# Hybrid decoder layer in split float32: one of the four weight-block sums of a block pair made by an accumulating transfer

## What is computed

```
x <- LN(alpha*x + 0.5*SwiGLU_pre(x))          # w_gate, w_up: 1024 x 2816, w_down: 2816 x 1024
x <- LN(alpha*x + W_out[attention(x) || conv group(x)])
x <- LN(alpha*x + 0.5*SwiGLU_post(x))
swiglu(x) = (silu(x @ wg) * (x @ wu)) @ wd
```

## Time and profile before

| | us |
|---|---|
| median of 3 runs | 1032.84 |
| lowest, highest | 1032.51, 1033.01 |
| the profiled execution's own time | 1032.17 |
| its span in the profile | 1030.4 |
| PE busy | 990.4 (96%) |
| DVE busy | 687.4 (67%) |
| ACT busy | 466.8 (45%) |
| POOL busy | 69.8 (7%) |

### The profile page before, as it was taken

The page is one execution under the profiler, slowest core; times in us unless marked ns, Lnnn a source line. Parts: engine busy times, 40 slices in busy tenths (PEclk is TensorE's granted clock), DMA queues, the critical chain, the costliest instruction groups (busy, mean ns, idle before and its releaser), DMA issues.

```text
span 1030.4 us, 18173 instructions
## 1 busy us (share of the span) xinstructions
PE 990.4 (96%) x7538; PEld 967.2 (94%) x7538; DVE 687.4 (67%) x984; ACT 466.8 (45%) x780; POOL 69.8 (7%) x80
## 2 busy tenths in 40 slices
PE   8979999999999999999999998979999999999994
PEld 8979999999999999999888998979999999999994
DVE  5788742577886468726667687988634587784456
ACT  4455531245445235546555456644521354553230
POOL 2000000000000000107142000000000000000004
PEclk9999999999999999999999999999999999999998
DMA  9255333123225344362022463042432222336402
GB/s 259 83 122 141 108 119 103 42 88 119 82 83 167 100 123 83 100 191 82 23 62 83 133 188 97 28 131 79 132 104 62 83 82 83 103 117 184 146 1 87
DMA packets 131594, 108.19 MB, mean 105 GB/s; under 512 B 13138, under 2 KB 129590, under 8 KB 131496
## 3 DMA queue, kind: packets, MB, share of 16 engines
q1 hardware_dynamic: 130368, 105.46, 34.5%
q10 hardware_dynamic: 1144, 1.57, 1.2%
HBM read 103.08 MB, written 4.95 MB: 105 GB/s over the span
## 4 chain that ended last, share of the span: by engine, by line
PE 71%; DVE 18%; ACT 6%; issue 4%; DMA 0%; DVEq 0%; POOL 0%; ACTq 0%; SPq 0%
PE banks L1057 26%; PE banks L1070 24%; PE banks L880 15%; DVE w_lo L1814 4%; DVE more_raw L1806 2%; DVE w_raw L1806 2%; ACT w_hi L1380 2%; DVE w_sum L1806 2%; PE banks L1242 1%; DVE w_lo L1783 1%; DVE ln_sq L1923 1%; DVE more_lo L1814 1%; ACT w_hi L1366 1%; ACT x_hi L1515 1%; PE banks L1288 1%
## 5 line engine op out<-in xcount | busy, mean ns | idle before, releaser
L1070 PE MATMUL banks<-h_hi,w_hi 128*128 128x280 f32 (+1 forms) x480 | 139.1, 290 | 0.0
L1070 PE MATMUL banks<-h_hi,w_lo 128*128 128x280 f32 (+1 forms) x480 | 139.0, 290 | 0.0
L1070 PE MATMUL banks<-h_lo,w_hi 128*128 128x280 f32 (+1 forms) x480 | 138.8, 289 | 0.0
L880 PE MATMUL banks<-x_hi,w_hi 128*128 128x280 f32 (+1 forms) x416 | 126.1, 303 | 2.9 <-DVE x_lo L2159 0.9
L1057 PE MATMUL banks<-x_hi,w_hi 128*128 128x280 f32 (+1 forms) x400 | 117.9, 295 | 10.6 <-ACT ln_sq L1471 8.7
L880 PE MATMUL banks<-x_lo,w_hi 128*128 128x280 f32 (+1 forms) x416 | 120.6, 290 | 0.0
L880 PE MATMUL banks<-x_hi,w_lo 128*128 128x280 f32 (+1 forms) x416 | 120.5, 290 | 0.0
L1057 PE MATMUL banks<-x_hi,w_lo 128*128 128x280 f32 (+1 forms) x400 | 116.9, 292 | 0.0
L1057 PE MATMUL banks<-x_lo,w_hi 128*128 128x280 f32 (+1 forms) x400 | 116.8, 292 | 0.0
L1783 DVE TENSOR_TENSOR w_lo<-w_raw,w_hi 128x1024 fp32r<-128x1024 f32 (+1 forms) x66 | 77.9, 1183 | 57.6 <-ACT w_hi L1366 57.2
L1057 PE MATMUL banks<-t_hi,w_hi 128*128 128x280 f32 x336 | 98.3, 293 | 0.7 <-issue 0.7
(11 more groups left out here) (238 smaller groups left out, 2654.4 us busy)
## 6 DMA issues: line engine op xcount, KB each, us to landing
w_raw<-in_ffn_w_down SPq DMA_DIRECT2D x30, 512.0 KB, 4.1
more_raw<-in_ffn_w_down SPq DMA_DIRECT2D x28, 512.0 KB, 3.8
w_raw<-in_ffn_w_gate SPq DMA_DIRECT2D x24, 512.0 KB, 4.0
w_raw<-in_ffn_w_up SPq DMA_DIRECT2D x24, 512.0 KB, 5.0
more_raw<-in_ffn_w_gate SPq DMA_DIRECT2D x20, 512.0 KB, 4.0
more_raw<-in_ffn_w_up SPq DMA_DIRECT2D x20, 512.0 KB, 5.1
w_raw<-in_w_in SPq DMA_DIRECT2D x14, 512.0 KB, 4.5
w_raw<-in_w_out SPq DMA_DIRECT2D x32, 128.0 KB, 2.9
```

Of the source, the lines that this page charges most:

```text
L880: mm = nc.tensor.matmul(out[:, 0:n], w[:, t, :], x(k), start=(k == ends[0] and w is hi and x is rhs_hi), stop=(k == ends[1] and w is lo))
L1070: mm = nc.tensor.matmul(out, w[:, k - k0, c * P:(c + 1) * P], h[:, k, cols(half, f)], start=(k == 0 and w is hi and h is h_hi), stop=(ku = ...
```

## The change

S1 is no longer made by DVE. As soon as a21 has landed, POOL issues two transfers that read a22's bytes from DRAM again (256 KB each, two of the four rows of 1 KB of each partition) and add them to a21 in its buffer. DVE makes the other three sums from S1: S2 = S1 - a11, S3 = a22 - S2, S4 = a12 - S2. For j > 0 all three stand ahead of the lo half of step 2's weights. The loads by SP stay as they are, and PE's and ACT's order too.

```
@@ block_hi (ACT)
+                elif s == 3:
+                    act.wait_ge(s1_summed[j % 2], 32 * ((N_PAIRS * f + j) // 2 + 1))
                 else:
-                    act.wait_ge(blocks_summed, 4 * (N_PAIRS * f + j) + ({4: 1, 2: 2, 5: 3, 3: 4} if j == 0 else {4: 1, 3: 2, 2: 3, 5: 4})[s])
+                    act.wait_ge(blocks_summed, 3 * (N_PAIRS * f + j) + {2: 1, 4: 2, 5: 3}[s])
@@ block_sum (DVE)
-                if i == 0:
-                    dve.wait_ge(weights_in[RAW[n0, "21"]], ARRIVED[n0, "21"])
-                    out, a, b, op = a11, a11, a21, ALU.subtract
-                elif i == 1:
-                    dve.wait_ge(weights_in[RAW[n0, "22"]], ARRIVED[n0, "22"])
-                    out, a, b, op = a21, a21, a22, ALU.add
-                elif i == 2:
-                    dve.wait_ge(blocks_summed, 4 * q + 1)
-                    dve.wait_ge(weights_in[RAW[n0, "22"]], ARRIVED[n0, "22"])
+                if i == 2:
+                    dve.wait_ge(s1_summed[j % 2], 32 * (q // 2 + 1))
                     if BEFORE[n0 + 2] is not None:
                         dve.wait_ge(steps_done, FREE[BEFORE[n0 + 2]])
-                    out, a, b, op = s2, a22, a11, ALU.subtract
+                    out, a, b, op = s2, a21, a11, ALU.subtract
+                elif i == 0:
+                    dve.wait_ge(blocks_summed, 3 * q + 1)
+                    dve.wait_ge(weights_in[RAW[n0, "22"]], ARRIVED[n0, "22"])
+                    out, a, b, op = a11, a22, s2, ALU.subtract
                 else:
-                    dve.wait_ge(blocks_summed, 4 * q + (2 if j == 0 else 3))
+                    dve.wait_ge(blocks_summed, 3 * q + 1)
                     out, a, b, op = a12, a12, s2, ALU.subtract
@@ next_lo (DVE)
                 if s == 2 and j:
                     block_sum(f, j, 2)
+                    block_sum(f, j, 0)
                     block_sum(f, j, 3)
                 block_lo(f, j, s)
-                if s == 1 and j:
-                    block_sum(f, j, 0)
-                    block_sum(f, j, 1)
@@ gate_up_first (DVE), f == 0
-                    block_sum(f, 0, 0)
                     combination(f, 0)
...
                     hidden(f, 1, 0)
+                    block_sum(f, 0, 0)
                     block_sum(f, 0, 3)
@@ gate_up_first (DVE), f == 1, and both
-                    next_lo(n + 1)
+                    block_sum(f, 0, 0)
                     combination_lo(f, 1)
                     block_sum(f, 0, 3)
                 next_lo(n + 2)
                 combination_lo(f, 0)
-                block_sum(f, 0, 1)
                 hidden(f, 1, 1)
@@ feed_forward (DVE), f == 1, behind ln_sum_squares(3)
-                    block_sum(f, 0, 0)
+                    next_lo(U_GU[1] + 5)
@@ POOL
+            def second_row_sum(f, j):
+
+                key = (pair_unit(f, j), "21")
+                pool.wait_ge(weights_in[RAW[key]], ARRIVED[key])
+                w = w_up[0, f].rearrange("(k p) n -> p k n", p=P)
+                for k in range(0, QT, 2):
+                    nc.gpsimd.dma_start(raw(key, QT)[:, k:k + 2, :], w[:, QT + k:QT + k + 2, (2 + 2 * j) * P:(4 + 2 * j) * P],
+                                        accum_op=ALU.add).then_inc(s1_summed[j % 2], 16)
+
             for n in range(4):
                 weight_lo(n)
+            for j in range(N_PAIRS):
+                second_row_sum(0, j)
...
+            second_row_sum(1, 0)
             ln_sum_squares(3)
+            for j in range(1, N_PAIRS):
+                second_row_sum(1, j)
```

More of the change, by code:

```diff
@@ L456, in build @@
         blocks_summed = sem("blocks_summed")
+        s1_summed = [sem(f"s1_summed{i}") for i in range(2)]
         p1_copied = sem("p1_copied")
```

## The result

| | before | after |
|---|---|---|
| median of 7 runs each, us | 1032.84 | 1036.29 |
| lowest, highest | 1031.50, 1034.82 | 1034.74, 1038.49 |
| ratio, with its 95% interval | | 1.0030 (1.0017 to 1.0043) |
| profiled execution, and its span | 1032.17, 1030.4 | 1034.87, 1033.1 |
| DVE busy, POOL busy | 687.4, 69.8 | 666.0, 118.5 |

The account below looks back on a forecast made before the run. PE was taken to wait for DVE's order of work, which loses one operation per pair. Terms -6.0, -5.9 and +4.9 gave -7.0 us, from the median 1032.84 to 1025.8 us; range 1021.8 to 1031.5.

Parts of the forecast that it names:

- Pair 0: First pair of each f: without the sum on DVE, PE's step 6 starts 3.0 us earlier; -6.0 us together.
- The later pairs: Step 6 of fourteen later pairs: PE's stall for DVE's step 4 addition goes, 0.42 us each; -5.9 us.
- rival 2: Later pairs' stalls stay, by the wait for step 3 or slower DVE operations; 1031 to 1032 us; 9%.
- Pair 2 of f=0: Crowded stretch beside ACT's transfer: a22 lands late, PE stalls 3.4 us, the lower clock adds 1.5; +4.9 us.
- the clock's part: After the long stall ahead of pair 1's step 6 at f=0, PE's clock drops to the lower level; 1.5 us.
- Rival 4: Pair 2 of f=0: accumulating packets take 0.3 us, S1 comes at 96, stall 13.3; slower, 1035.7 us; 9%.

Follow-up runs that it names:

- e6: Changed kernel, but S1 of pair 2 of f=0 alone made by DVE from the landed a22, without POOL's transfers; 1024.98 us, ratio 0.9915.
- e5: Changed kernel, but ACT's transfer of 992 rows issued at step 3 of pair 0 of f=0, when pair 2's loads are nearly through; 1037.87 us, ratio 1.004.
- e3: Changed kernel with POOL's transfers as plain copies of a22 over a21, without the addition; 1035.46 us in one execution.
- e4: Changed kernel with S1 made by four transfers of 128 KB in place of two of 256 KB; 1037.35 us in one execution.
- e1: Changed kernel with ACT's transfer of 992 rows issued later, at the start of pair 2 of f=0; 1021.43 us, ratio 0.9868.
- e8: Changed kernel with ACT's 992 rows at their old place, but split into four transfers of 248 rows; 1036.04 us, ratio 1.0004.
- e7: Changed kernel with ACT's rows issued at step 3 of pair 0 of f=0, as four transfers of 248 rows; 1032.0 us, ratio 0.9965.

## Why the prediction was wrong

**Pair 0: right.** -3.0 for each f was forecast. Measured: -2.8 at f=0 (66.69 against 69.45; -3.1 without the late start), -3.1 at f=1 (the lag falls from 8.7 to 5.6). The two parts are right too: at step 5 of f=1 the lag is 6.8 (679.96 against 673.20), so 1.9 us come up to there and 1.1 behind it.

**The later pairs: right.** -0.42 for each of the seven in an f: at f=1 the lag falls from 5.6 to 2.7, 2.9 us. DVE's sums wait for PE's steps thirteen times, 4.2 us in all and 0.3 at the most, and take 1.23 us each, as before (rows of L1806 above), so the doubt of rival 2 didn't come true. Two transfers in a quiet stage take 9 us, not over 23.

**Pair 2 of f=0: the step that failed.** I wrote that S1 "lands at about 83 to 84 and does not decide", and that a22, at 87.2, does. Measured: a22 landed at 84.8 (57.8 and 27.0 us), S1 at 95.6, 12 us later than I had it. (For a22 I had added 3.2 us for POOL's packets ahead of it; it landed 0.8 later than the 84.0 without them. That e6 comes so near the forecast, with a22 used from 87.1 and a wait of 3.1 for my 87.2 and 3.4, is luck: none of POOL's packets for pair 2 move there, five operations of DVE and not four stand behind a22, and PE was 2.7 us later than I had it.) Two assumptions about S1 carried the error, and both were put down as if they cost nothing:

- *That both halves are in flight together.* They run one after the other. From POOL's issue behind a21's landing (77.94) two quiet transfers in a row take 9 us, to 86.9. By this alone the addition would end 5.4 us later, at 92.3, and PE would wait 4.2 us: little more than the 3.4 of the forecast, and no change of sign.
- *That POOL's packets take turns with the others, or better.* Its queue got nothing on the eight engines of ACT's transfer. That delayed the first transfer by 13.0 - 4.4 = 8.6 us, and 86.9 + 8.6 = 95.5. This is what turned the sign.

e5 shows the second without late loads, and e3 and e4 show a third way to the same place: where a21 itself lands at 85 to 86, ACT's rows are all but through, and the transfers in series, beside the rest of SP's late loads, bring S1 to 93.6 and 97.2. All three ways were seen only with ACT's transfer in that stretch; e1 takes it away and has 1021.4.

In the sum the term stood at +4.9. It measures 9.65 + 2.8 + 0.4 = 12.8 us at step 6 of pair 1 (the 0.4 is this pair's own gain), and the clock's part comes on top: of the 9.65 us of lag, six later pairs at 0.42 take 2.5 back, which leaves 7.1, and 8.7 are there at the start of the f=1 block, 1.6 more. I had 1.5. The granted clock in that stretch (89.2 to 92.2, 92.2 to 101, 101.2 to 104.2 us; PEclk is the third figure from the end):

```profile
89.20:92.20 3.00, 0.00 (x0) 0.00 (x0) 0.00 (x0) 0.00 (x0) 0.98 (x1) 0.80 0.52 163
92.20:101.00 8.80, 0.00 (x0) 0.00 (x0) 5.34 (x6) 2.01 (x2) 1.91 (x3) 0.50 0.45 66
101.20:104.20 3.00, 3.00 (x13) 3.00 (x14) 1.61 (x2) 1.35 (x2) 0.57 (x1) 0.50 0.60 82
```

It falls within PE's idle time and is still at the lower level, 1.2 GHz, when step 6 begins. The length of a wait alone doesn't tell the level behind it: here PE waited 2.36 us ahead of step 5 of pair 0, less than the 2.5 us that left the clock at 1.00 before the change, and from 60.7 to 63.6 us the granted clock was 0.50. 12.8 + 1.6 in place of 4.9 is 9.5 us more, and -7.0 + 9.5 = +2.5, against +2.7 between the profiled executions.

**Rival 4 had the numbers and not the cause.** It gave S1 at 96, the addition's end at 101.4, a wait of 13.3 and 1035.7 us; measured are 95.6, 101.0, 12.55 and 1036.3. But it paid for them with packets of 0.3 us, and a packet took 0.11. Its 9% were too few because I asked only what a packet costs, and not what else can keep a transfer from landing.

**The Trainium skill's rule** ("DMA: Bandwidth & Descriptors", "Queues, rings and completion order"), which I had read as speaking for many of POOL's descriptors in a turn, was read from one side only: what lets POOL's queue hold an engine lets ACT's hold it as well. The trace agrees with turns of one row only for a queue that is already being served; for one that comes new, e5 shows 12 us without any. The price of the Trainium skill for a transfer (the same page, "Anatomy of one DMA — SWDGE (gpsimd) path"), 2.6 us by its formula, an estimate, is too low here: 4.4 us each.

## What to carry to other kernels

Moving a sum from an engine to a transfer traded 1.2 us behind the last load for a whole latency behind it (4.4 us here), and for as many as are in series: look for the one place where a load lands just in time, since here it decided the sign, and leave that place as it was (e6) or clear it (e1). Where another queue holds the engines with one long transfer, cost a new transfer at the end of a long wait and not at a share of the turns. A transfer that nobody needs for 60 us should go where nothing lands just in time.

## What the runs showed of the hardware that was not expected

- A queue that starts on an engine in which ACT's long transfer of rows is running gets no packet for a long while: 12 us in e5 (65 to 77), whole stretches in the changed kernel (82 to 86), while a queue with work there all the time gets every second packet. Beside a backlog of SP's loads alone it got none from 86 to 89 us in e8. What sets the length isn't settled.
- POOL's accumulating transfers of 256 KB are issued one at a time, each when the one before has landed; of 128 KB pieces three go at once (e4), and of plain copies of 256 KB two (e3). In packets that is 272, 432 (three of 144) and 160 (two of 80), and 544 and 576 did not go: a limit between 432 and 544 packets would fit, an estimate that no run tested.
- An accumulating packet of 1 KB takes 0.11 us, ACT's row of 1.5 KB 0.21, a load's packet of 1 KB 0.045.
- ACT's issue of four transfers in a row held it for 8 to 10 us (e7, e8), where its one transfer of the same bytes took 1.3.
- Loads behind ACT's transfer land at quite different times in different executions: a21 at 77.6 after the change and at 86.3 in e3, issued 1.3 us later. Why isn't known.
